# One decoder layer on one core: the first load of activations and weights cut into two transfers

## The reference

```python
def reference(x, mem, w_in, ...):
    mix = _hybrid_mixer(x, w_in, w_gate_up, b_gate, gla_norm_g, w_mix_o)  # proj = x @ w_in, then both attentions
    x = _layer_norm(DEEPNORM_ALPHA * x + mix, ln1_g, ln1_b)
    xa = _mem_xattn(x, mem, w_xq, w_xkv, w_xo)
    x = _layer_norm(DEEPNORM_ALPHA * x + xa, ln2_g, ln2_b)
    ff = jnp.square(jax.nn.relu(x @ w_ff1)) @ w_ff2
    return _layer_norm(DEEPNORM_ALPHA * x + ff, ln3_g, ln3_b)
```

## Time and profile before

| | |
|---|---|
| median of three runs | 397.1 us (396.5 to 397.4) |
| the profiled execution's own time | 396.17 us |
| its span, first to last instruction | 394.3 us |
| TensorE busy | 387.2 us, 98% |
| VectorE, ScalarE, GpSimd busy | 347.3, 261.6, 80.3 us |
| mean granted TensorE clock | 0.995 of full |

### The profile page before, as it was taken

The page is one execution under the profiler, slowest core; times in us unless marked ns, Lnnn a source line. Parts: engine busy times, 40 slices in busy tenths (PEclk is TensorE's granted clock), DMA queues, the critical chain, the costliest instruction groups (busy, mean ns, idle before and its releaser), DMA issues.

```text
span 394.3 us, 5662 instructions
## 1 busy us (share of the span) xinstructions
PE 387.2 (98%) x2087; PEld 331.3 (84%) x2087; DVE 347.3 (88%) x450; ACT 261.6 (66%) x345; POOL 80.3 (20%) x79
## 2 busy tenths in 40 slices
PE   9999999999999999999999999999999999999993
PEld 6888888888988888889988888888888888888882
DVE  5699595899989786969798898999999999999997
ACT  6666568656554638447673658888888777778830
POOL 2049400047870205000004300000000000000003
PEclk9999999999999999999999999999999999999998
DMA  8998737743656281563737465677777677777002
GB/s 282 380 383 277 254 102 250 258 153 109 234 191 213 67 301 64 213 214 119 229 123 304 133 219 150 218 231 240 230 226 235 207 231 225 235 233 228 16 2 106
DMA packets 25313, 79.70 MB, mean 202 GB/s; under 512 B 1766, under 2 KB 3398, under 8 KB 21190
## 3 DMA queue, kind: packets, MB, share of 16 engines
q1 hardware_dynamic: 22592, 74.98, 54.5%
q0 software_dynamic: 2160, 3.93, 5.7%
q10 hardware_dynamic: 534, 0.43, 0.4%
HBM read 78.28 MB, written 1.05 MB: 201 GB/s over the span
## 4 chain that ended last, share of the span: by engine, by line
PE 98%; DVE 1%; issue 0%; DVEq 0%
PE bank L1650 17%; PE bank L1651 17%; PE bank L1652 17%; PE bank L2035 13%; PE bank L1709 13%; PE bank L1713 7%; PE bank L2042 7%; PE bank L1861 2%; PE bank L1656 1%; PE bank L1701 1%; PE bank L1815 1%; PE bank L1848 0%; PE bank L1914 0%; PE bank L1963 0%; PE bank L1807 0%; PE bank L1806 0%
## 5 line engine op out<-in xcount | busy, mean ns | idle before, releaser
L1060 DVE TENSOR_TENSOR w_lo<-raw,w_hi 128x2048 fp32r<-128x2048 f32 x30 | 70.6, 2360 | 6.9 <-ACT w_hi L643 6.9
L643 ACT CAST w_hi<-raw 128x2048 fp32r<-128x2048 f32 x32 | 60.7, 1912 | 13.5 <-PE bank L1652 11.1
L2035 PE MATMUL bank<-actA,w_hi 128*128 128x512 f32 x224 | 55.5, 390 | 0.0
L2035 PEld LDWEIGHTS bank<-actA,w_hi 128*128 128x128 f32 x224 | 42.0, 188 | 8.7
L605 POOL DMA_DIRECT2D raw<-in_w_ff x15 | 13.2, 877 | 156.6 <-DMA raw<-in_w_ff 156.6
L1650 PE MATMUL bank<-w_hi,actB 128*128 128x512 f32 x107 | 42.7, 399 | 0.0
L1651 PE MATMUL bank<-w_lo,actB 128*128 128x512 f32 x107 | 41.9, 391 | 0.0
L1652 PE MATMUL bank<-w_hi,actB 128*128 128x512 f32 x107 | 41.8, 391 | 0.0
L1709 PE MATMUL bank<-actA,w_hi 128*128 128x512 f32 x156 | 38.2, 392 | 0.0
L1650 PE MATMUL bank<-w_hi,actA 128*128 128x512 f32 x96 | 38.0, 396 | 0.0
L1652 PE MATMUL bank<-w_hi,actA 128*128 128x512 f32 x96 | 37.5, 391 | 0.0
(11 more groups left out here) (244 smaller groups left out, 868.5 us busy)
## 6 DMA issues: line engine op xcount, KB each, us to landing
raw<-in_w_ff SPq DMA_DIRECT2D x32, 1024.0 KB, 5.2
raw<-in_w_in SPq DMA_DIRECT2D x10, 1024.0 KB, 7.7
raw<-in_w_xkv SPq DMA_DIRECT2D x8, 1024.0 KB, 5.0
raw<-in_w_mix_o SPq DMA_DIRECT2D x4, 1024.0 KB, 4.7
raw<-in_w_xq SPq DMA_DIRECT2D x4, 1024.0 KB, 4.9
raw<-in_w_xo SPq DMA_DIRECT2D x4, 1024.0 KB, 4.7
raw<-in_w_ff POOLq DMA_DIRECT2D x15, 256.0 KB, 5.0
raw<-in_lead SPq DMA_DIRECT2D x6, 384.0 KB, 5.1
```

Source lines behind the costliest of these rows:

```text
L643: act.copy(dst, half_view(u)).then_inc(hi_done, 1)
L1060: dve.tensor_tensor(dst, half_view(u), hi_part.bitcast(f32), ALU.subtract).then_inc(lo_done, 1)
L2035: pe.matmul(b[:, :].rearrange("p (h s) -> p h s", h=2), hi[:, k, m * P:(m + 1) * P], actA[:, :, k, :], start=k == 0, stop=False, skip_grou ...
```

## The change

The transfer for k = 0 is cut in two. The first piece has x and the first 256 weight columns (256 KB, 2 KB in each partition), the second the other 256 columns (128 KB, 1 KB in each partition). Each has its own semaphore, so there are eight lead loads instead of seven; the third cut of k = 0 waits for the second piece, and all later cuts name a load whose number is one higher. `WGLR_BEHIND` goes from 5 to 6, so that `wglr` stays between the load of k = 5 and the load of k = 6 and 7. The transfers are written as slices of a three-dimensional view of `lead`. Casts, subtractions and matmuls are the same in number, size and order.

```diff
-EARLY_LOADS = [(0, 1), (1, 2), (2, 3), (3, 4), (4, 5), (5, 6), (6, 8)]
 EARLY_ROW = S + 512
-EARLY_CUTS = [(0, 0, 1, 0, S), (0, 0, 1, S, S + 256), (0, 0, 1, S + 256, EARLY_ROW)]
+EARLY_LOADS = [(0, 1, 0, S + 256), (0, 1, S + 256, EARLY_ROW)]
+EARLY_LOADS += [(k0, k1, 0, EARLY_ROW) for k0, k1 in ((1, 2), (2, 3), (3, 4), (4, 5), (5, 6), (6, 8))]
+EARLY_CUTS = [(0, 0, 1, 0, S), (0, 0, 1, S, S + 256), (1, 0, 1, S + 256, EARLY_ROW)]
 for _k in range(1, 6):
-    EARLY_CUTS += [(_k, _k, _k + 1, 0, S), (_k, _k, _k + 1, S, EARLY_ROW)]
-EARLY_CUTS += [(6, 6, 8, 0, S), (6, 6, 7, S, EARLY_ROW), (6, 7, 8, S, EARLY_ROW)]
-WGLR_BEHIND = 5
+    EARLY_CUTS += [(_k + 1, _k, _k + 1, 0, S), (_k + 1, _k, _k + 1, S, EARLY_ROW)]
+EARLY_CUTS += [(7, 6, 8, 0, S), (7, 6, 7, S, EARLY_ROW), (7, 7, 8, S, EARLY_ROW)]
+WGLR_BEHIND = 6
...
-            for n, (k0, k1) in enumerate(EARLY_LOADS):
-                sp.dma_start(early_raw[:, k0:k1, :].rearrange("p k n -> p (k n)"),
-                             lead[:, k0 * EARLY_ROW:k1 * EARLY_ROW]).then_inc(early_in[n], 16)
+            lead_rows = lead.rearrange("p (k n) -> p k n", n=EARLY_ROW)
+            for n, (k0, k1, a, b) in enumerate(EARLY_LOADS):
+                sp.dma_start(early_raw[:, k0:k1, a:b], lead_rows[:, k0:k1, a:b]).then_inc(early_in[n], 16)
```

## The result

The kernel after takes 398.27 us, the median of seven runs (397.91 to 398.82); the kernel before took 396.67 beside it (396.39 to 397.41). The ratio is 1.0034, with a 95% interval of 1.0025 to 1.0043 (the two medians alone would give 1.0040): slower by 1.0 to 1.7 us, beyond the 0.2% that can be told from no change, and beyond the range that was forecast. One execution of the kernel before, among those beside the second group of experiments ("other cuts" to "other addresses"), took 486.4 us at a mean granted clock of 0.753 and is left out of their ratios.

A forecast was written before the change was run, and what follows sets the result against it. TensorE's queue was taken to bound the kernel; up to 0.17 us gained at the first matmul would be lost at k = 1, held by load 1 at +0.05. The median was forecast at 397.1 us, range 396.4 to 397.9.

The forecast's parts named there:

- What bounds the kernel: Whole kernel: TensorE, busy 387.2 of 394.3 us, sets the time, which moves only if its queue begins earlier or is held.
- The first landing: Load 0's first piece, 128 KB less: lands 0.3 us earlier, at 4.05, within a gain of 0 to 0.40.
- The first matmul: Start of k = 0: warm-up frees TensorE at 4.73, gain at most 0.17 us, 0.10 or less left if spacing is wide.
- The second piece: Load 0's last 256 weight columns: lands at 4.35 to 4.45, its cast ends at 4.86, hidden.
- One more issue on SyncE's queue: Loads behind load 0: every later issue moves by 0.43 us, covered by a lead of more than 2 us.
- Shorter pieces: Load 0's 2 KB and 1 KB rows: +0.05 us for load 1 and all behind it, bounded by -0.05 and +0.15.
- The form of the last lead load: Last lead load written as three-dimensional: costed at 0, since w_in is read so too and streams at 400 GB/s.
- The sum: k = 1 starts at 6.34 against 6.29, held by load 1, +0.05 us; span 394.3 or 394.4, median 397.1; chance 0.50.
- the third: Stream behind load 0 starves between small pieces: load 1 lands 0.42 to 0.84 us later, median 397.5 to 397.9; chance 0.10.
- Rivals 1 and 2: At k = 1, gain kept, 0.06 to 0.17 us earlier, chance 0.17; first piece lands only at 4.3, time unchanged, chance 0.15.

The follow-up runs named there:

- other cuts: The changed kernel with load 0 cut at 128 or at 384 weight columns instead: 398.25 us, ratio 1.0027, and 398.70 us, ratio 1.0040.
- other addresses: The changed kernel with lead laid out k outermost in HBM, rows of one load 3 KB apart, not 24 KB: 397.75 us, ratio 1.0012.
- the pause: The kernel before, uncut, with SyncE waiting behind load 0 for a GpSimd memset that ends at 1.58 us: 397.81 us, ratio 1.0018.
- two small transfers: The kernel before with two extra transfers of 32 bytes in each partition behind load 0: 399.16 us, ratio 1.0057.
- change again: The changed kernel run once more, unaltered, for a second profile: 398.06 us, ratio 1.0021 to the kernel before.
- load 1 on ScalarE: The changed kernel, both pieces of load 0 on SyncE's queue, but load 1 issued by ScalarE's queue: 397.11 us, ratio 0.9999.
- view only: The kernel before, uncut, with its seven lead loads written as slices of the three-dimensional view: 397.03 us, ratio 0.9996.
- x first: The changed kernel cut elsewhere, x alone first (128 KB), then all 512 weight columns (256 KB): 396.99 us, ratio 0.9998; again 397.42 us, 1.0001.
- small behind load 0: The kernel before, uncut, with an unused extra transfer of 64 bytes in each partition behind load 0: 398.19 us, ratio 1.0023.

## Why the prediction was wrong

- **What bounds the kernel**: right. TensorE's queue sets the end, and a delay at k = 2 went through to the end undiminished in the profiles (1.88 at k = 2, 1.89 at k = 7, 1.9 in the span).
- **The first landing**: right in sign, too small. 0.62 us earlier, not 0.3. The forecast held the ramp for fixed and only took bytes off; but with load 1 issued later, load 0 also has the engines to itself. In the five profiles with load 0 whole and load 1 issued at 1.15 to 1.17, its first cast starts at 4.35 to 4.64; in the four with load 0 whole and load 1 issued later (the pause among them) at 3.90 to 4.04, with no byte taken off.
- **The first matmul**: 4.52 and not 4.73 for the weight load. The warm-up leaves TensorE free earlier than its last record suggests. But the gain was lost again at once: the forecast let two matmuls run at the wide spacing, in the profile nearly all twelve of k = 0 did, and k = 1 began 0.74 later than before. The wait for load 2 covered that.
- **The second piece**: hidden, as forecast.
- **One more issue on SyncE's queue**: this is the step that failed. "0.43 of a lead of more than 2 us is covered" took the time between a load's issue and its landing for slack. It is not slack: the pause moves the issues of loads 1 and 2 by 0.4 us, touches nothing else, and costs 0.7 us (0.18%); two small transfers move them by 0.9 and cost 2.3 (0.57%). The price was put at 0. With load 2 issued at its old time the cut costs nothing (ratio 0.9999), so this term is the result, though the pause alone gives only 0.7 of its 1.4 us.
- **Shorter pieces**: near 0, as forecast; the same rows with the old issue times lose nothing.
- **The form of the last lead load**: nothing, as forecast.
- **The sum**: k = 1 was to be held by load 1 at +0.05. Load 1 came 0.37 late (0.85 in the second profile), and load 2, where 0.33 of slack was counted, 2.2. The prediction named as a sign of being wrong that the stream behind load 0 moves by more than 0.3 us, and so it did.
- **The rivals**: the third had the right kind of mechanism, a stream that runs dry between transfers, and the wrong place and price. It looked at load 1 alone, priced 0.42 to 0.84 us, and argued it away with "its engines are not free of load 0 until over 3". That is true, and load 1 was only 0.4 late; load 2, the next one behind it, paid 2.2. Its chance was put at 0.10. Rivals 1 and 2 did not come: no gain was kept, and the first piece landed early.

The record of semaphore signals says more about load 2. Each load raises its semaphore by 16, in sixteen signals with a time each, and is used when the last has come. The signals of load 2, in us, with its issue:

| kernel | issued | first | twelfth | last |
|---|---|---|---|---|
| before | 1.63 | 5.41 | 5.98 | 6.29 |
| load 1 on ScalarE | 1.62 | 5.49 | 6.15 | 6.37 |
| view only | 1.62 | 5.67 | 6.24 | 7.07 |
| x first | 2.08 | 5.69 | 6.28 | 6.68 |
| pause | 2.00 | 5.81 | 6.53 | 7.50 |
| small behind load 0 | 2.10 | 5.56 | 7.24 | 8.05 |
| the change | 2.10 | 5.53 | 7.34 | 8.51 |
| change again | 2.10 | 5.86 | 7.08 | 8.57 |

So load 2 isn't late as a whole: its first sixteenth comes 0.1 to 0.5 us later than before, its last 2.2 or more. What the late issue brings is a spread, in which some sixteenths fall far behind the others. Such a straggler also appears once without any delay (view only: fifteen signals by 6.46, the last at 7.07), so one landing in one profile may be off by more than half a microsecond. That each signal stands for one of the 16 DMA engines fits their number; the trace doesn't name the engine.

Why some parts fall behind is not settled. Shown is that, but for x first, the loss follows the issue time of load 2 (none when it keeps its time, with or without the cut), that it grows with the delay, and that it moves on to load 3 or back to load 1 as the delay does. Not shown is what the engines wait for while five loads are queued, and a late issue of load 1 alone was not tried. Open too is why x first doesn't lose, though its load 2 is issued as late as in the change: its first transfer is the shortest, 128 KB, and its loads 1 and 2 are both only 0.3 to 0.5 us late. And the addresses may have changed half of the loss, which nothing here explains.

The Trainium skill, page DMA: Bandwidth & Descriptors, section Issuing engines are not separate DMA queues, says that issuing from several engines saves only the sequencer's time to start a DMA, usually small beside the transfer. The runs agree on the size, 0.43 us beside 3.6 us and more from issue to landing, and show that this small time can be all there is to win or lose: an issue taken off SyncE's queue took away the whole loss of 1.4 us.

## What to carry to other kernels

At the start of a kernel, while the first transfers ramp up, the time at which the next loads are issued can be on the critical path even if they land microseconds later; here it was that of load 2. A delay can cost more than itself: 0.4 us of pause cost 0.7 us, 0.43 us of an extra issue 0.9 (the small transfer) to 1.4 (the change). Before a first load is cut, count what each issue behind it is moved by, and put the extra one on another engine's queue or behind the loads that are needed next; here both took the loss away. And the gain has to have somewhere to go: here load 1, a transfer of its own with no slack, held the second step, and the cut with load 2's issue time restored gained nothing (ratio 0.9999).

## What was not expected of the hardware

The matmuls of k = 0 are 0.21 us apart in some executions and 0.12 in others, with the same warm-up and a granted clock that reads 1.00, full speed, in both. In the profile after, the first four weight loads begin at 4.52 and the next four at 5.38, and k = 1 begins at 7.03: 2.51 us for k = 0, before 1.42. In the second profile of the same kernel the spacing is 0.12 from 5.26 on. Here a wait for a load followed and hid it. With the form of the transfers alone changed nothing hid it: k = 0 ran from 4.96 to 7.08, no wait followed, and the span was 395.1 us, 0.8 longer than before, with no loss over ten runs. A comparison of single profiles of a start should allow for a microsecond of this.

An issue on SyncE's queue can be held up as well: that of the last lead load took 1.54 us in the profile after and 1.20 in the second, in place of 0.45.
